# A deeper row ring (eight buffers for seven, eleven for ten) and selection temporaries kept for one head

## The reference

```python
def one_block(hb):
    q = (hb @ w_pq).reshape(PEER_BLOCK, PEER_HEADS, 2, PEER_HALF)
    s1 = jnp.einsum("thd,hkd->thk", q[:, :, 0], sub_keys1).astype(jnp.float32)
    s2 = jnp.einsum("thd,hkd->thk", q[:, :, 1], sub_keys2).astype(jnp.float32)
    v1, i1 = lax.top_k(s1, PEER_TOPK)
    v2, i2 = lax.top_k(s2, PEER_TOPK)
    cand = (v1[..., :, None] + v2[..., None, :]).reshape(...)
    ...
    top_s, pos = lax.top_k(cand, PEER_TOPK)
    idx = jnp.take_along_axis(cand_idx, pos, axis=-1)
    g = jax.nn.softmax(top_s, axis=-1).astype(hb.dtype)
    u = jnp.take(expert_u, idx, axis=0)
    act = jax.nn.gelu(jnp.einsum("thkd,td->thk", u, hb))
    vv = jnp.take(expert_v, idx, axis=0)
    return jnp.einsum("thk,thkd->td", g * act, vv)
```

## Time and profile before

| | |
|---|---|
| Time, median of three runs | 2109.81 us |
| Profiled execution, and its span | 2108.62 us, 2106.8 us |
| Mean granted TensorE clock | 0.951 |
| Busy TensorE, VectorE, ScalarE, GpSimd | 1687.1, 1220.3, 708.0, 599.9 us |
| Moved by DMA | 718.50 MB |
| Gathered rows among it | 604.02 MB |

### The profile page before, as it was taken

How to read it: one execution, slowest core, us unless ns; L and a number is a source line. 1 busy time by engine, 2 the same in 40 slices (tenths; PEclk the granted TensorE clock), 3 DMA queues, 4 the chain that set the end, 5 groups by cost and what they waited for, 6 DMA issues and landing times.

```text
span 2106.8 us, 22263 instructions
## 1 busy us (share of the span) xinstructions
PE 1687.1 (80%) x7420; PEld 765.7 (36%) x7420; DVE 1220.3 (58%) x3172; ACT 708.0 (34%) x2204; POOL 599.9 (28%) x584
## 2 busy tenths in 40 slices
PE   5899998599787997989957777767777776877776
PEld 2775897445453444444421221112121121211111
DVE  2434216766764563458756777767777765554554
ACT  2225202123772322243223333343333333333332
POOL 0000000033223332322324443435443443333331
PEclk7999999799778999999989999999999999999999
DMA  9455632299769897978949999999999999999996
GB/s 399 157 198 210 245 120 79 84 418 415 303 241 352 354 396 323 402 299 354 291 173 422 422 421 421 421 421 416 422 421 422 421 421 393 422 421 421 422 421 277
DMA packets 102467, 718.50 MB, mean 341 GB/s; under 512 B 13584, under 2 KB 13584, under 8 KB 15696
## 3 DMA queue, kind: packets, MB, share of 16 engines
q0 software_dynamic: 82944, 604.02, 70.4%
q1 hardware_dynamic: 18544, 110.69, 13.4%
q10 hardware_dynamic: 864, 2.36, 0.3%
HBM read 712.30 MB, written 4.73 MB: 340 GB/s over the span
## 4 chain that ended last, share of the span: by engine, by line
DMA 43%; PE 34%; DVE 12%; issue 5%; ACT 4%; POOL 1%; SPq 0%; DVEq 0%; POOLq 0%; ACTq 0%
DMA ring<-in_expert_uv_dram,uidx 41%; PE ps L797 8%; PE ps L540 7%; PE ps L659 6%; DVE ring L1437 4%; PE ps L680 3%; PE ps L665 2%; PE ps L720 1%; POOL ring L415 1%; PE ps L536 1%; PE ps L512 1%; DMA ring<-in_wpack_dram 1%; PE ps L570 1%; PE ps L603 1%; ACT wsel L1044 1%
## 5 line engine op out<-in xcount | busy, mean ns | idle before, releaser
L797 PE MATMUL ps<-ring,wdiag 128*32 128x512 f32 x2304 | 863.3, 632 | 246.7 <-ACT wdiag L1049 227.8
L1437 DVE CUSTOM_DVE_ANT_0 ring<-ring,mA 128x1024 f32<-128x1024 f32 x576 | 702.4, 1224 | 529.7 <-DMA ring<-in_expert_uv_dram,uidx 525.4
L415 POOL DMA_INDIRECT ring<-in_expert_uv_dram,uidx x576 | 598.6, 1039 | 1426.2 <-PE ps L797 990.2
L797 PEld LDWEIGHTS ps<-ring,wdiag 128*32 128x32 f32 x2304 | 173.3, 113 | 882.1 <-ACT wdiag L1049 542.4
L1042 ACT ACTIVATE gel<-act_in 128x1 f32<-128x1 f32 x576 | 116.8, 203 | 891.0 <-DVE act_in L1437 890.4
L1049 ACT ACTIVATE wdiag<-repeat,wsel 128x32 f32<-128x32 f32 x576 | 185.1, 321 | 18.9
L1044 ACT ACTIVATE wsel<-gel,gsel 128x1 f32<-128x1 f32 x576 | 169.6, 295 | 18.7
L540 PE MATMUL ps<-hB,ring 128*128 128x384 f32 x320 | 108.8, 492 | 0.0
L720 PE MATMUL ps<-hB,ring 128*128 128x384 f32 x256 | 89.3, 501 | 8.5 <-issue 8.5
L659 PE MATMUL ps<-hB,ring 128*128 128x384 f32 x256 | 91.3, 513 | 5.5 <-DVE kv L1278 5.5
L540 PEld LDWEIGHTS ps<-hB,ring 128*128 128x128 f32 x320 | 59.1, 190 | 42.1 <-issue 5.5
(11 more groups left out here) (233 smaller groups left out, 1599.1 us busy)
## 6 DMA issues: line engine op xcount, KB each, us to landing
ring<-in_wpack_dram SPq DMA_DIRECT2D x96, 1024.0 KB, 8.7
ring<-in_expert_uv_dram,uidx POOLq DMA_INDIRECT x576, 20.4
xB<-in_x_b_dram SPq DMA_DIRECT2D x2, 1536.0 KB, 18.4
o_y_p<-mA ACTq DMA_DIRECT2D x16, 128.0 KB, 5.4
bias<-in_bias_dram SPq DMA_DIRECT2D x1, 1024.0 KB, 29.8
o_v_p<-kv SPq DMA_DIRECT2D x4, 256.0 KB, 7.5
o_k_p<-xB SPq DMA_DIRECT2D x4, 256.0 KB, 13.7
xB<-in_keysT_dram SPq DMA_DIRECT2D x1, 1024.0 KB, 7.7
```

The costliest lines, as they stand in the source:

```text
L415: nc.gpsimd.indirect_dma_start(out=ring[:, slot, :], out_offset=None, in_=ins["expert_uv"], in_offset=bass.IndirectOffsetOnAxis(ap=uidx[:, ...
L797: mm = nc.tensor.matmul(pY[c * GT:(c + 1) * GT, half, :], wdiag[:, n % NDIAG, :], ring[:, ROW[n][0], D + half * 512:D + (half + 1) * 512], ...
L1437: nc.vector.tensor_tensor_reduce(r, r, h2n[:, g % 2, :], 1.0, 0.0, ALU.mult, ALU.add, act_in[:, g % 2, j:j + 1]).then_inc(s["dot"], 1)
```

## The change

NROW goes from 7 to 8, and with it NSLOT from 10 to 11. The six temporaries of the selection are kept for one head; the instructions that use them are the same in number and size.

```diff
-NROW = 7
+NROW = 8
 NSLOT = NRING + NROW
...
-        val = sb("val", [P, 2 * PH, TOPK])
-        idx = sb("idx", [P, 2 * PH, TOPK], U32)
-        idxf = sb("idxf", [P, 2 * PH, TOPK])
+        val = sb("val", [P, 2, TOPK])
+        idx = sb("idx", [P, 2, TOPK], U32)
+        idxf = sb("idxf", [P, 2, TOPK])
         top = sb("top", [P, PH, TOPK])
-        pos = sb("pos", [P, PH, TOPK], U32)
-        posu = sb("posu", [P, 2, PH, TOPK], U32)
-        posf = sb("posf", [P, 2, PH, TOPK])
+        pos = sb("pos", [P, TOPK], U32)
+        posu = sb("posu", [P, 2, TOPK], U32)
+        posf = sb("posf", [P, 2, TOPK])
...
-                    for m in ms:
-                        cd.did(nc.vector.max(val[:, m, 0:8], sc[:, m, :]))
+                    for m in sides:
+                        cd.did(nc.vector.max(val[:, m, 0:8], sc[:, m0 + m, :]))
...
-                    cd.did(nc.vector.tensor_copy(posf[:, :, hd, :], posu[:, :, hd, :]))
+                    cd.did(nc.vector.tensor_copy(posf[:, :, :], posu[:, :, :]))
```

More of the change, by code:

```diff
@@ L1304, in pick_head @@
                     cleft = rest
-                    ms = range(m0, m1)
+                    sides = range(2)
                     settle()
                     stand()
-                    for m in ms:
-                        cd.did(nc.vector.max(val[:, m, 0:8], sc[:, m, :]))
+                    for m in sides:
+                        cd.did(nc.vector.max(val[:, m, 0:8], sc[:, m0 + m, :]))
                     settle()
                     stand()
-                    for m in ms:
-                        cd.did(nc.vector.max_index(idx[:, m, 0:8], val[:, m, 0:8], sc[:, m, :]))
-                        cd.did(nc.vector.match_replace(lf[:, m - m0, :], val[:, m, 0:8], sc[:, m, :], -3.0e38))
+                    for m in sides:
+                        cd.did(nc.vector.max_index(idx[:, m, 0:8], val[:, m, 0:8], sc[:, m0 + m, :]))
+                        cd.did(nc.vector.match_replace(lf[:, m, :], val[:, m, 0:8], sc[:, m0 + m, :], -3.0e38))
                     yield
@@ L1317, in pick_head @@
                     stand()
[L1318 to L1319 removed]
+                    for m in sides:
+                        cd.did(nc.vector.max(val[:, m, 8:16], lf[:, m, :]))
                     settle()
                     stand()
[L1322 to L1323 removed]
+                    for m in sides:
+                        cd.did(nc.vector.max_index(idx[:, m, 8:16], val[:, m, 8:16], lf[:, m, :]))
                     settle()
[L1325 removed]
+                    cd.did(nc.vector.tensor_copy(idxf[:, :, :], idx[:, :, :]))
                     cd.did(nc.vector.tensor_tensor(cand.rearrange("p (a b) -> p a b", a=TOPK),
[L1327 removed]
+                                                   bc(val[:, 0, :], 2, TOPK), bc(val[:, 1, :], 1, TOPK), ALU.add))
                     yield
@@ L1333, in pick_head @@
                     stand()
-                    cd.did(nc.vector.max_index(pos[:, hd, 0:8], top[:, hd, 0:8], cand))
+                    cd.did(nc.vector.max_index(pos[:, 0:8], top[:, hd, 0:8], cand))
                     cd.did(nc.vector.match_replace(cleft, top[:, hd, 0:8], cand, -3.0e38))
@@ L1350, in pick_head @@
                     for side in range(2):
-                        cd.did(nc.vector.tensor_tensor(e4, bc(posf[:, side, hd, :], 2, TOPK), bc(iota16[:, :], 1, TOPK),
+                        cd.did(nc.vector.tensor_tensor(e4, bc(posf[:, side, :], 2, TOPK), bc(iota16[:, :], 1, TOPK),
                                                        ALU.is_equal))
                         settle()
-                        cd.did(nc.vector.tensor_tensor(e4, e4, bc(idxf[:, m0 + side, :], 1, TOPK), ALU.mult))
+                        cd.did(nc.vector.tensor_tensor(e4, e4, bc(idxf[:, side, :], 1, TOPK), ALU.mult))
                         settle()
```

12 lines of the change are left out of this document (3 added, 9 removed).

## The result

The kernel after takes 2090.82 us (median of four runs, 2089.02 to 2091.76), the kernel before, run beside it, 2110.38 (2107.15 to 2113.86). The ratio is 0.9906, with an interval of 0.9888 to 0.9924: 19.6 us faster, where 40 were forecast. The time lies within the outer bounds of 2040 and 2100 us and just above the forecast's own range of 2050 to 2090; the direction was right, and the gain was half of what was forecast.

A forecast was written before the change was run, and what follows sets the result against it. Before 1127 us the seven-buffer row ring was taken to put a whole round on the path of every four folds; after it, the DMA's pace binds. Terms 12 + 5 + 10 + 2 + 8 + 3 = 40 us gave 2069 us, range 2050 to 2090.

The forecast's parts named there:

- nothing lost in A: Before 420 us, eleven buffers for A's weights change nothing: 0, bounds 0 and 2 us of loss.
- the queue: Rival, 640 to 900 us: the eighth row delays each of 16 weight blocks by 2.5 us; 2110 to 2130 us; chance 0.06.
- The round goes off the path: Up to fetch 192: with eight buffers rows leave one round, some 14 us, earlier, more than median landing, dot and scalar work.
- The signs that the prediction named: Mostly 520 to 900 us: row waits more than halved, rate about 375 GB/s; dense work ending some 35 us earlier.
- Attention, 12 forecast: 520 to 640 us: half of TensorE's 25.2 us idle time won, 12 us; bounds 0 and 25.
- 640 to 760 us, 5 forecast: End of attention and merge: 5 us won from fold waits and broken folds; bounds 0 and 8.
- 760 to 900 us, 10 forecast: Merge and projection, with the `place` at fetch 116: 10 us won; bounds 0 and 15.
- 900 to 960 us, 2 forecast: Around B's second normalisation, whose 8.5 us wait stays: 2 us won; bounds 0 and 2.
- 960 to 1127 us, 8 forecast: VectorE leads; half the fold waits, some 6 us, and one more row, 2.5 us: taken as 8; bounds 0 and 21.
- Late places, 3 forecast: After fetch 192, at the `place` of 308 and 436: one more row covers dips, 3 us; bounds 0 and 4.6.
- TensorE was the pace all along: Rival, before 1127 us: only 24.3 us of fold waits are the rows'; 2101 us or no change at 2108; chance 0.18.
- the 22 us that a full clock would have given: 520 to 640 us: clock granted at 0.77; full, it would save 22 us beyond the 12; not counted in the forecast.

The follow-up runs named there:

- early8: Kernel after, but ten buffers instead of eleven for A's weights and from fetch 192 on; eight row buffers before that: 2087.8 us, ratio 0.987 to before.
- temps7: Kernel before, seven and ten buffers kept, with only the selection's temporaries cut to one head: 2112.8 us, ratio 1.0008 to before.
- pairsat7: Kernel before, seven buffers, folding in twos instead of fours only between fetches 35 and 67 (attention): 2098.8 us, ratio 0.994 to before.
- drain7: Kernel before, seven buffers, VectorE finishing the selection three fetches earlier for tile groups 1, 3 and 4: 2107.73 us, ratio 0.9946 to before.
- drain8: Kernel after, eight buffers, VectorE finishing the selection three fetches earlier for tile groups 1, 3 and 4: 2085.61 us, ratio 0.984 to before.
- onehead7: Kernel before without the selection of seven of B's eight heads for tile group 2 (other outputs): 2099.41 us, ratio 0.9936 to before.
- onehead8: Kernel after without the selection of seven of B's eight heads for tile group 2 (other outputs): 2072.9 us, ratio 0.9805 to before.
- pairs7: Kernel before, seven buffers, folding in twos instead of fours wherever the fetch number is odd: 2126.52 us, ratio 1.0054 to before.
- best8: Kernel after plus tile group 2's `place` one fetch later, selection ended early at the other places, twos in attention: 2067.13 us, ratio 0.9775 to before.

## Why the prediction was right in its direction and wrong in its size

**Right: what bounds.** Only the time before 1127 us could be won, and only the row ring up to fetch 192 wins it; `early8` and `temps7` show both. After fold 191 the kernels differ by 0.3 us in 969.

**Right: nothing lost in A, and no queue.** TensorE got no wait for B's weight blocks, and the rival "the queue" did not come: fold 67 to 139 became 8.3 us shorter and not longer.

**"The round goes off the path": in part. This is the step that failed.** The prediction let it go because a round of 14 us is longer than the median landing of 10.1 us with a dot and the scalar work. But the landing is not a fixed time. In after, rows that took 16.26, 15.73 and 15.40 us from issue to landing stand on the chain at 737, 798 and 852 us, in stretches where the DMA moves 421 to 424 GB/s. They are fetches 99, 116 and 131, and the same three took 12.06, 16.39 and 10.65 us in before. Fetches 99 and 131 are of the kind 4k+3 that the eighth buffer lets go early: they left 1.2 us behind their predecessors in place of 5.6 and 7.7, and took 4.2 and 4.8 us longer to land. The full DMA took back most of the 4.3 and 6.5 us. The chain from fold 3 to fold 191, of before and then of after, has the landings with the same share of it, 129 of 695 and 134 of 676 us; from 520 to 900 us alone it fell from 84 to 65.

```profile
by line: DMA ring<-in_expert_uv_dram,uidx 18.6%; PE ps L797 12.5%; PE ps L659 11.4%; PE ps L540 7.6%; issue 7.1%; PE ps L680 5.0%; PE ps L720 4.1%; DVE ring L1437 3.6%; PE ps L665 3.5%; POOL ring L415 2.4%; DMA o_v_p<-kv 1.8%; PE ps L603 1.
```
```profile
by line: DMA ring<-in_expert_uv_dram,uidx 19.8%; PE ps L797 11.9%; PE ps L659 11.0%; issue 10.0%; PE ps L540 7.0%; DVE ring L1437 4.1%; POOL ring L415 3.8%; PE ps L680 3.6%; PE ps L665 3.5%; PE ps L720 3.1%; PE ps L603 1.8%; PE ps L570 1.6%
```

The signs that the prediction named say the same. VectorE's waits for rows from 520 to 900 us fell by a quarter (124.0 to 92.4 us) and not by more than half; TensorE's fold waits from 24.3 to 18.4 us and not under 12; the `place` of 116 waits 10.73 us and not under 3; the rate from 520 to 900 us rose from 341 to 359 GB/s and not to 375; fold 191 ends 19.0 us earlier and not 35. Nor did the rate stay and the waits only change their names, as the sign of being wrong had it.

**Attention, 12 forecast, 7.5 measured.** 13 us could be won there (`pairsat7`), by twos that shorten the round and the block of folds both. The eighth buffer took VectorE's waits for rows (15.6 to 6.5 us) and left the wait for ScalarE's copies nearly as it was (13.7 to 12.5).

**640 to 760 us, 5 forecast, 3.7 measured.** Within the spread.

**760 to 900 us, 10 forecast, 4.6 measured. Here that step cost most.** The text gave the 9.5 us at the `place` of fetch 116 to the late row and had them go with one more buffer. The wait stayed (10.73 us): row 116, behind which it stands, took 16.39 us to land in before and 15.73 in after, as the rows shared a full DMA with tokens, keys and weights. `drain7` and `drain8` take it away and win the missing 5 to 6 us. The ceiling of 15 us by the rate was not passed, and said nothing of which edit reaches it.

**900 to 960 us, 2 forecast, 0.8 lost.** The work there is B's second normalisation with no row on its path. The difference of 2.8 us is small, and why it is a loss stays open; before alone has 46.8 us where five variants with seven buffers have 48.5 to 50.1.

**960 to 1127 us, 8 forecast, 5.7 measured.** The row that the longer ring holds at the `place` of 180 gave its 2.1 us (179 to 191), near the 2.5 of the sum. The fold waits gave 3.6 in place of some 6: VectorE leads there, as the text said, and its seven selections keep 13 us at either depth (`onehead7`, `onehead8`). Half of the fold waits was a choice, and no run says why it is a third less.

**Late places, 3 forecast, 0.3 measured.** From 1400 to 1440 and from 1700 to 1760 us the rate rose from 414 to 420 and from 395 to 401 GB/s, which is 1.4 us by the method of the forecast, but the folds show 0.3. `early8`, with ten buffers there, shows none either (968.7). A likely reason, not shown, is that a mean rate over a stretch counts holes that the landing of the rows, one in 2.49 us, does not wait for.

The rival "TensorE was the pace all along" named the missing part better than its price: waits were renamed, as `pairs7` shows outside of attention. Of the 22 us that a full clock would have given in attention little came: the granted clock rose from 0.77 to 0.82, and to 0.87 in `best8`, with the stops of the chain still there. The Trainium skill, "TensorE: Matmul & The Clock Gate", section HAM oscillation, has the clock fall again and again where waits for DMA interrupt the work; the trace agrees in part only, as VectorE's waits for rows in that stretch fell from 15.6 to 6.5 us and the clock rose to 0.82 only, beside 23 us of TensorE idle for other engines.

## What to carry to other kernels

Before a wait is priced at its length, ask whether the thing waited for is late because it was asked for late (a buffer, which depth mends) or because the resource is full (which it doesn't), and look for the cost in the idle DMA behind the wait. Consumers that take their inputs in groups hold the buffers for the whole group: in attention depth and smaller groups won the same time. The step from six to seven buffers paid 50 us and that from seven to eight 20, so a gain is not carried on from one depth to the next. And the time from issue to landing is not a constant of the row: beside a full DMA it grows with what is in flight.

## What the runs showed of the hardware

- Four matmuls of one fold (128x512, 32 columns of weights each) take 1.90 us, sixteen of four folds 1.94 us. A group's busy time goes by runs and clock and not by matmuls: 152.1, 145.3 and 223.5 us for the same 752, in 63, 60 and 101 runs. Busy TensorE can hide a wait in this way, 9 us in one stretch of 106.
- A second full queue stretched the distance between two rows from 2.49 to 4.96 and 5.47 us at an unchanged 425 GB/s in all.
- The same row landed 12.06 us after its issue in before and 16.26 in after, another 10.65 and 15.40, each time with the DMA at 420 to 427 GB/s; the least between 520 and 960 us in before is 5.4 us.
- 24 table loads of 1.28 us each in 120 us on a ScalarE that was busy 73% cost nothing that could be measured.
- Profiles of unchanged stages differ by up to 8 us in attention (133.1 to 141.3 us with seven buffers), and only by 1.2 us from fold 99 to 139. A forecast of a stage from one profile has at least that error.
